# Second block's expert outputs: gated at the PSUM copy and added to the output rows by the scatter, in place of a separate combine

## What is computed

```python
h2 = rms_norm(x, norm_ffn[l])
x = x + hier_moe_2(h2, ...)

# hier_moe_2: group softmax picks 1 of 4 groups, then the best 2 of its 8 experts
weights = g_p[:, None] * e_p                      # one gate for each of a token's two experts
combine = jnp.sum(one_hot(expert_idx) * weights[..., None], axis=1)
for e in range(32):
    he = silu(hf @ w_gate[e]) * (hf @ w_up[e])    # 1024 -> 256
    y = y + combine[:, e:e+1] * (he @ w_down[e])  # 256 -> 1024
```

## Time and profile before

| | us |
|---|---|
| median of 3 runs (1504.05 to 1507.62) | 1504.61 |
| the profiled execution, its own time | 1505.68 |
| span of the profiled execution | 1503.8 |
| TensorE busy in the span | 1288.5 (86%) |
| VectorE, ScalarE, GpSimd busy | 703.1, 462.1, 421.1 |
| mean DMA rate over the span | 174 GB/s |
| mean granted TensorE clock | 0.925 of full |

### The profile page before, as it was taken

How to read it: one execution, slowest core, us unless ns; L and a number is a source line. 1 busy time by engine, 2 the same in 40 slices (tenths; PEclk the granted TensorE clock), 3 DMA queues, 4 the chain that set the end, 5 groups by cost and what they waited for, 6 DMA issues and landing times. The chain is left out here.

```text
span 1503.8 us, 20161 instructions
## 1 busy us (share of the span) xinstructions
PE 1288.5 (86%) x7568; PEld 1030.9 (69%) x7568; DVE 703.1 (47%) x1271; ACT 462.1 (31%) x1011; POOL 421.1 (28%) x358
## 2 busy tenths in 40 slices
PE   7997789949999439899999999999888948999782
PEld 6776467839999329778989978788676844554440
DVE  5797773634343474763762636673124351111112
ACT  4542343223233144443242243433222311111110
POOL 5355211211010205312423324134323302332213
PEclk9999779959999769999999999999989968999996
DMA  7300350169996422301221303322113489999995
GB/s 265 112 0 1 129 208 31 42 245 379 373 387 249 131 88 77 113 1 32 87 71 71 112 30 112 115 64 77 56 58 115 184 356 364 418 419 419 419 385 184
DMA packets 65285, 262.33 MB, mean 174 GB/s; under 512 B 8456, under 2 KB 18312, under 8 KB 52384
## 3 DMA queue, kind: packets, MB, share of 16 engines
q1 hardware_dynamic: 54176, 233.73, 40.5%
q0 software_dynamic: 9216, 21.00, 4.0%
q10 hardware_dynamic: 1792, 6.29, 1.2%
HBM read 242.04 MB, written 29.43 MB: 181 GB/s over the span
## 5 line engine op out<-in xcount | busy, mean ns | idle before, releaser
L1703 POOL TENSOR_TENSOR block_w_lo<-block_w,block_w_hi 128x512 fp32r<-128x512 f32 x96 | 130.4, 1361 | 219.8 <-ACT block_w_hi L1681 219.8
L241 PE MATMUL dil_bank<-block_w_hi,xT_hi 128*128 128x512 f32 x288 | 116.8, 406 | 4.3 <-PEq L830 4.3
L2380 PE MATMUL e_gu<-e_w,e_xT 128*64 128x256 f32 x896 | 105.8, 390 | 15.3 <-DMA e_w<-in_gu 14.6
L1681 ACT ACTIVATE block_w_hi<-block_w 128x512 fp32r<-128x512 f32 x96 | 60.4, 631 | 182.9 <-PE dil_bank L243 117.5
L242 PE MATMUL dil_bank<-block_w_lo,xT_hi 128*128 128x512 f32 x288 | 115.0, 399 | 0.0
L243 PE MATMUL dil_bank<-block_w_hi,xT_lo 128*128 128x512 f32 x288 | 114.9, 399 | 0.0
L2380 PEld LDWEIGHTS e_gu<-e_w,e_xT 128*64 128x64 f32 x896 | 63.9, 140 | 48.9 <-DMA e_w<-in_gu 16.5
L241 PEld LDWEIGHTS dil_bank<-block_w_hi,xT_hi 128*128 128x128 f32 x288 | 77.6, 269 | 8.8 <-issue 4.7
L242 PEld LDWEIGHTS dil_bank<-block_w_lo,xT_hi 128*128 128x128 f32 x288 | 77.8, 270 | 4.0
L243 PEld LDWEIGHTS dil_bank<-block_w_hi,xT_lo 128*128 128x128 f32 x288 | 77.6, 269 | 4.3
L2442 DVE TENSOR_TENSOR e_prod<-e_sg,e_gu 128x128 f32<-128x128 f32 x32 | 9.2, 287 | 140.4 <-ACT e_sg L2473 140.4
(11 more groups left out here) (506 smaller groups left out, 3116.1 us busy)
## 6 DMA issues: line engine op xcount, KB each, us to landing
e_w<-in_gu SPq DMA_DIRECT2D x44, 2048.0 KB, 18.0
e_w<-in_dn SPq DMA_DIRECT2D x48, 1024.0 KB, 19.9
block_w<-in_w_dil SPq DMA_DIRECT2D x9, 2048.0 KB, 8.1
block_w<-in_w_out SPq DMA_DIRECT2D x4, 2048.0 KB, 9.0
block_w<-in_w_gates SPq DMA_DIRECT2D x4, 2048.0 KB, 9.0
w_t<-in_w_in_t SPq DMA_DIRECT2D x12, 512.0 KB, 3.5
slot_rows<-blank SPq DMA_DIRECT2D x12, 512.0 KB, 6.3
slot_rows<-e_y ACTq DMA_DIRECT2D x16, 384.0 KB, 8.9
```

The lines of the kernel that those rows point to most:

```text
L241: pe.matmul(out, lhs[0], rhs[0], start=first, stop=False)
L1681: act.activation(wh[:, j % RING, 0:width[i]], k.w[:, slot, c, 0:width[i]], ACT.Copy).then_inc(hi_ready, 1)
L1703: pool.tensor_tensor(wl[:, j % RING, 0:width[i]], k.w[:, (q0 + i) % 2, c, 0:width[i]], wh[:, j % RING, 0:width[i]].bitcast(F32), ALU.subtr ...
L2380: ins = pe.matmul(gubank[t % 2][g * S:(g + 1) * S, 0:2 * FG], xT[t % 2][:, turned_at(c):turned_at(c) + S], w1_piece(slot.of[t], w, 2 * FG) ...
```

## The change

1. `out_rows` of the second block: GpSimd stores each finished residual tile to `out` (four DMAs of 512 KB), with a semaphore `residual_out`.
2. `route`: `y_of` with its three VectorE steps goes. The `tok_of` step is moved ahead of the six steps for `slot`, `exp_of` and `used`. New is `gate_of`, the gate of each slot: two VectorE multiplies, 32 small matmuls with the one-hot tables that `tok_of` was made from, and a copy.
3. ScalarE's copy from PSUM takes `gate_of` as its scale.
4. The scatter goes to `out` by `tok_of` and adds (`compute_op=ALU.add`). A token can stand in two tiles, so scatter t now waits until scatter t - 1 has landed, where it waited for t - 2; scatter 0 waits for the residual.
5. `Combine` is deleted: no `slot_rows` gathers, no adds, no final store by SyncE. The block ends when the last two scatters have landed.

```diff
@@ out_rows, GpSimd
+                if residual is not None:
+                    for tt in range(TT):
+                        pool.wait_ge(row_ready, tt + 1)
+                        pool.dma_start(residual[tt * P:(tt + 1) * P, :], x1[:, tt, :]).then_inc(k.residual_out, 16)
@@ route, TensorE
+                if k.gate_of is not None:
+                    pe.wait_ge(hot_ready, 2)
+                    for j in range(2 * TT):
+                        i, tt = divmod(j, TT)
+                        for g in range(GROUPS):
+                            ins = pe.matmul(gbank[g * S:(g + 1) * S, 0:NT], ohr[:, i, tt, :], hot[:, i, tt, :], start=(j == 0),
+                                            stop=(j == 2 * TT - 1))
+                    ins.then_inc(gates_done, 1)
@@ route, VectorE: tok_of is taken here, ahead of slot, exp_of and used
-                if k.y_of is not None:
-                    step(dve.tensor_scalar(empty[:], tbank[:, 0:NT], -0.5, float(NO_ROW), ALU.is_gt, ALU.mult))
-                    step(dve.scalar_tensor_tensor(empty[:], k.c("iota")[:, 0:NT], 2.0 * S, empty[:], ALU.mult, ALU.add))
-                    step(dve.tensor_scalar(k.y_of[:], empty[:], k.c("half_row"), None, ALU.add))
+                if k.gate_of is not None:
+                    for i in range(2):
+                        dve.tensor_tensor(hot[:, i], hot[:, i], bc(k.gate[:, i], 2, NT), ALU.mult).then_inc(hot_ready, 1)
+                    dve.wait_ge(gates_done, 1)
+                    step(dve.tensor_copy(k.gate_of[:], gbank[:, 0:NT]))
@@ experts_moving, GpSimd
                     pool.wait_ge(y_s, t + 1)
-                    if t >= 2:
-                        pool.wait_ge(y_out[t % 2], 16 * (t // 2))
-                    pool.indirect_dma_start(halves, bass.IndirectOffsetOnAxis(ap=k.y_of[:, t:t + 1], axis=0), y[t % 2][:],
-                                            None, bounds_check=GROUPS * SLOTS - 1, oob_is_err=False).then_inc(
-                                                y_out[t % 2], 16)
+                    if t >= 1:
+                        pool.wait_ge(y_out[(t - 1) % 2], 16 * ((t - 1) // 2 + 1))
+                    else:
+                        pool.wait_ge(k.residual_out, 16 * TT)
+                    pool.indirect_dma_start(sums, bass.IndirectOffsetOnAxis(ap=k.tok_of[:, t:t + 1], axis=0), y[t % 2][:],
+                                            None, bounds_check=GROUPS * SEQ - 1, oob_is_err=False,
+                                            compute_op=ALU.add).then_inc(y_out[t % 2], 16)
@@
-                pool.sem_inc(tail.stored, 1)
-                tail.gather(pool)
@@ experts_moving, VectorE, ScalarE, SyncE
-                tail.add(dve)
-                    act.activation(y[t % 2][:], ybank[t % 2][0:U, :], ACT.Copy).then_inc(y_s, 1)
+                    act.activation(y[t % 2][:], ybank[t % 2][0:U, :], ACT.Copy, scale=k.gate_of[:, t:t + 1]).then_inc(y_s, 1)
-                tail.store(sp)
```

More of the change, by code:

```diff
@@ L1323, in row_stats, with out_rows @@
     return dve.bn_stats(stats[:, half, :], x[:, half * 512:(half + 1) * 512])
-def out_rows(k, name, src, xT, tmp, vecs, loads, router, lg, rows, finished, scale=None, gain_cols=None, early=None, over_rows=None):
+def out_rows(k, name, src, xT, tmp, vecs, loads, router, lg, rows, finished, scale=None, gain_cols=None, early=None, over_rows=None, residual=None):
     nc, x1 = k.nc, k.x1
@@ L1818, in route @@
         ohj = k.sb(s, f"{name}_ohj", [P, 2, TT, NT])
[L1819 to L1822, removed]
+        hot = k.sb(s, f"{name}_hot", [P, 2, TT, NT])
+        rbank, totals, tbank, gbank = (k.ps(s, f"{name}_{n}") for n in ("rbank", "totals", "tbank", "gbank"))
+        (step_d, diff_ready, exp_ready, m_ready, rank_done, oh_ready, tok_done, bits_ready, xg_ready, tok_ready, hot_ready,
+         gates_done) = (
+            k.sem(f"{name}_{n}") for n in ("step", "diff", "exp", "mready", "rank", "oh", "tok", "bits", "xg", "tokready",
+                                           "hot", "gates"))
         with nc.Block() as block:
@@ L2240, in __init__, with experts_moving @@
         self.last = [max([u for u in range(t) if self.of[u] == self.of[t]], default=None) for t in range(NT)]
-def experts_moving(k, name, E, S, x_in, rows, w_gu, w_dn, out_rows, weights, late, tail):
+def experts_moving(k, name, E, S, x_in, rows, w_gu, w_dn, out, weights, late):
     nc = k.nc
@@ L2486, in _ @@
                 every_tile(act, used, tile)
[L2489 to L2497, removed]
-        for j in range(2 * TT):
-            k.gathered[4 + j] += 16
-    def gather(self, pool):
-        pool.wait_ge(self.stored, 1)
-        for j in range(2 * TT):
-            tt, i = divmod(j, 2)
-            pool.indirect_dma_start(self.rows[j], None, self.out_rows, bass.IndirectOffsetOnAxis(
-                ap=self.k.slot[:, i, tt:tt + 1], axis=0)).then_inc(self.row_in[j], 16)
-    def add(self, dve):
-        x = self.x
-        for tt in range(TT):
-            for i in range(2):
-                j = 2 * tt + i
-                dve.wait_ge(self.row_in[j], self.row_base[j] + 16)
-                dve.scalar_tensor_tensor(x[:, tt, :], self.rows[j], self.k.gate[:, i, tt:tt + 1], x[:, tt, :],
-                                         ALU.mult, ALU.add).then_inc(self.used, 1)
-                dve.wait_ge(self.used, j + 1)
-    def store(self, sp):
-        for tt in range(TT):
-            sp.wait_ge(self.used, 2 * tt + 2)
-            sp.dma_start(self.out[tt * P:(tt + 1) * P, :], self.x[:, tt, :]).then_inc(self.out_done, 16)
-        sp.wait_ge(self.out_done, 16 * TT)
 class CombineAndNorm:
@@ L3282, in second_block @@
                  early=load_early,
-                 over_rows=load_over_rows)
+                 over_rows=load_over_rows, residual=d["out"])
     stage.close()
@@ L3307, in second_block @@
         w1.append([k.w1_over_consts, k.sb(s, "e2_w1_6b", [P, 3 * 2 * FF])])
-        experts_moving(k, "e2", E2, S2, k.gather_sems[2:4], d["rows"], d["gu2"], d["dn2"], slots, weights, late,
-                       Combine(k, "c2", slots, w1[2:4], k.x1, d["out"]))
+        experts_moving(k, "e2", E2, S2, k.gather_sems[2:4], d["rows"], d["gu2"], d["dn2"], d["out"], weights, late)
 def first_block(k):
```

32 lines of the change are left out of this document (15 added, 17 removed).

## The result

| | before | after |
|---|---|---|
| median, us | 1505.91 | 1546.38 |
| lowest and highest | 1504.05 to 1507.62 | 1543.73 to 1554.63 |
| runs on the same chip | 4 | 4 |
| profiled execution, its own time | 1505.68 | 1546.12 |

The ratio is 1.027, with a 95% interval of 1.0243 to 1.0297: 40 us slower, where 6 or 7 were forecast and 1487 to 1560 was the range. The new wait does what the forecast said of it, but several of the numbers around it were too small. The time lies in the range because the range was drawn wide enough for the slow-add rival too; the forecast's own case was 1504 to 1524.

What follows compares the result with a forecast made beforehand. The prediction took the experts as bound by weight loads, then by scatters in series: 1315 + 22 P, with P = 8.85 after removing the combine, gives span 1509.8; plus 1.9 it is 1511.7, said as 1512, range 1487 to 1560.

Steps and rivals of the forecast that it cites:

- slow-add rival: Expert scatters: reading, adding and writing take 2 to 3 us more each, P about 11, time 1559; above 1524, chance 0.25.
- the forecast's own case: Scatters in series set the experts' pace: P 8.5 to 9.4, 1504 to 1524 us, residual delay included; chance 0.50.
- What bounds the kernel before: Experts' stage: it ends with the weights, the last arriving at 1466.7, with the DMA engines full from 1254 to 1460.
- What goes: End of the kernel: the combine is all on the path, 24.2 us; if nothing else moved, the span would be about 1480.
- The new wait: Expert scatters: each waits for the one before, so the period is landing plus about 0.8 us, 9.2 at full load.
- P: Period from one expert scatter to the next in series, taken as 8.85 us; each 0.1 us is 2.2 us of time.
- The discount for gaps in the load: Expert scatters: engines idle 8% of the time let waiting scatters land early, so P drops from 9.2 to 8.85 us.
- The addition in the engines: DMA engines during the experts: an add also reads its destination, 0.3 us a tile, 10 us over 32.
- third rival: DMA engines: the add's read costs twice 0.3 us a tile but no latency; P 8.8 or more, 1511 to 1518.
- The residual store: Before the experts: 2.1 MB, 5.1 us, hides in two later DMA gaps of 3.7 and 2.2 us; without them 5 us.
- Scatters do not bind: Expert scatters: landings average below 7.2 us, P below 8.0, weights set the end; 1482 to 1500 us, chance 0.25.
- The fourth: Before the experts: the residual store holds up `token_rows` by its full 5 us with no gap, shifting everything to 1517.

Runs made afterwards that it cites:

- b_add: The kernel before with the scatter adding to slot_rows instead of copying, old wait for t - 2 and combine kept: 1519.06 us, ratio 1.0074.
- a_turns: The changed kernel with experts taken in turn from the four groups, so scatter t waits for t - 2 only: 1503.14 us, ratio 0.9965.
- b_serial: The kernel before with only the wait changed: plain scatter t waits for scatter t - 1, combine kept: 1534.05 us, ratio 1.0173.
- a_plain: The changed kernel without the addition: scatters copy to the output rows, still in series: 1521.87 us, ratio 1.0087.
- b_serial_add: The kernel before with both the adding scatter and the wait for t - 1, combine kept: 1560.33 us, ratio 1.0354.
- a_turns_serial: The changed kernel with experts in turn from the four groups, but the wait for t - 1 kept: 1548.94 us, ratio 1.0257.
- a_turns_no_residual: a_turns without the four residual stores and scatter 0's wait for them, so the output lacks the residual: 1503.02 us, ratio 0.9969.
- a_late_residual: The changed kernel with the residual stores moved into the routing, behind the gathers of tiles 0 and 1: 1549.63 us, ratio 1.0281.
- a_turns_all: a_turns_nowait plus left residual halves stored early by SyncE, which also waits for the last two scatters: 1499.88 us, ratio 0.995.
- a_turns_nowait: a_turns without SyncE's wait for the first gathered rows ahead of its last three first loads: 1503.41 us, ratio 0.9971.
- a_sp_end: The changed kernel with SyncE instead of GpSimd waiting for the last two scatters: 1543.82 us, ratio 1.0229.

## Why the forecast was right in direction and short in size

**What bounds the kernel before.** Right, by the way back: with two scatters allowed in flight and the addition in, the chain ends in weights again (b_add, a_turns), and the addition's DMA price of 13 us shows up there as 11 us of time.

**What goes, 24.2 us.** Right, as far as three pairs of runs can tell: one kernel of each has the combine, the other the residual store and the gates. What was gained, plus scatter 0's later place behind the last residual add, plus the new end of about 5 us: 12 + 4 + 5 from b_serial to a_plain, 13 + 6 + 6 from b_serial_add to after, 16 + 6 + 5 from b_add to a_turns, that is 21 to 27 us.

**The new wait.** The mechanism is right and is shown: alone it costs 26 us (b_serial); with adding scatters, all else equal, 46 (a_turns_serial against a_turns). "Landing + about 0.8" is 0.88. The plain period was taken as 8.9 at full load: measured 8.79 and 8.76. What was sized wrong is the next term, an adding scatter's landing. The forecast's + 0.3 us, near the plain rows "since queueing dominates", was + 1.0 (8.76 to 9.82, 8.79 to 9.73). That is 0.7 us of P, some 15 us of time. Of it, 0.58 is GpSimd's own: 1.59 us for the instruction where the earlier trace rows have 1.01. The rest is flight. It is there with the weights in as well, where a landing is 4.0 instead of the 2.9 of the earlier trace rows, of which again 0.58 is issue; it also puts scatter 31 later, as scatter 30 took 4.5 us to land.

The Trainium skill's fit (page "DMA: Bandwidth & Descriptors", section "Anatomy of one DMA — SWDGE (gpsimd) path") of 2.0 us plus bytes / 436e3 gives 2.3 us for 0.13 MB, an estimate. The adding scatters of after do not agree with it even when almost alone: 3.7 at least.

**The discount for gaps in the load.** The second wrong term: 9.2 was lowered to 8.85, because the engines would be idle 8% of the time and a waiting scatter would land early then. That is 0.35 us of P, 8 us of time. The idle share was overrated. By the same reckoning b_serial, 8.2 us of DMA work in a period of 8.79, should have gaps of 7%, and it has none (share 1.00). It moved 411 GB/s x 8.79 us = 3.6 MB in a period, not 3.41; by these bytes the weights of about 23 tiles go out during the 22 periods. In after it is 371 GB/s x 9.82 us, 3.6 MB again, or 9.1 us of work at b_add's 401 GB/s, an estimate, where the forecast had 8.5. So b_serial says nothing on what a gap is worth.

The gaps in after are real (0.96 busy, 371 GB/s), but do not shorten the flights evenly. The 22 steps go 12.2, 12.3, 11.7, 9.8, 6.8, 10.7, 7.1, 11.4, 7.6 and so on, long and short in turn. It is the long ones, above anything in the of before, that carry the mean. b_serial_add shows the same pattern; the plain scatters of b_serial do not (10.4, 8.5, 8.2, 8.2, 8.1, 7.3, 8.7). With such steps a median says little: it is 9.5 in after and 7.0 in b_serial_add, at periods of 9.82 and 9.73; the mean landing, period less 0.88, is 8.9 in both. The landings of b_serial_add up to 1455:

```profile
DMA to landing us min/median/max: 6.0/7.0/10.7
```

One reading is that a scatter which lands early lets a gather and a tile through, whose freed buffers bring a burst of loads in front of the next scatter. That was argued from the order of events and is not shown; no run fixed the load.

**The addition in the engines.** 0.3 us a tile was 0.41, in the third rival's direction. In after, where the engines are busy 0.96, it does not set the end; it is what b_add pays.

**Behind the wait.** "Gather n + 2 is queued behind scatter n - 3", 12.4 us to the down projection, then tiles at TensorE's pace: this held, 46.75 forecast and 45.8 measured.

**The residual store.** "They hide there", and "net zero, within 1" for the routing, together a start as before: wrong, it is 6.0 us later (6.6 with the shift of the whole kernel). There were gaps of 3.7 and 2.2 us, and the store fills both. But a gap is no free place if something behind it in the same queues is late by what fills it. `token_rows` lands later, the loads behind it go out at 1229.77 instead of 1225.49, and the backlog, which held the start already, ends at about 1249 instead of 1245. The forecast had each piece ("without that cover they would be 5 us"), and put the loads' delay "inside the second gap". a_turns_no_residual shows it is the stored bytes and not the routing; a_late_residual, that moving them behind the gathers does not help (46.8 instead of 44.1 to the first turn); a_turns_all, that moving half of them ahead into an idle stretch does (39.4). What event exactly releases the engines then stays open; a_turns_nowait excludes SyncE's wait for the gather.

**The end.** Not in the sum at all: 5.6 us lie behind the last landing, where the kernel before has next to nothing. Moving the wait to SyncE leaves 4.0 of them in the profile of a_sp_end and 5.0 in a_turns_all.

**Rivals.** Scatters do not bind: falls, mean landing 8.9 where it needed less than 7.2. Slow add: the time, 1546, lies in this case's field, above 1524, which had a chance of 0.25; by mechanism it is half as much as that case had (P 9.82 instead of about 11), and the rest of the way came mostly from the start and the end. The forecast's own case, P 8.5 to 9.4 and 1504 to 1524 with a chance of 0.50, failed by its own sign. The fourth, the residual store holding up `token_rows`, happened as well, in addition to the rest and not in its place: terms of the same sign added up, where the forecast had treated them as alternatives. That the 1546 fell inside the range is owed to the width given for rivals, not to the sum: of the 34.5 us missing in the span, 21 are the period, 7 the start and 6 the end.

## What to carry to other kernels

A wait that puts small DMAs in series beside a saturating stream costs landing plus 0.9 us each, here 8.8 us plain and 9.5 to 9.8 adding, while the same DMAs with two in flight keep up with 7 us a tile at an even longer flight. So look for an order in which neighbours touch different rows before paying for the wait (46 us between a_turns_serial and a_turns).
The rule that makes the wait necessary for neighbours that do share rows is in the Trainium skill, page "DMA: Bandwidth & Descriptors", section "Rules for kernel authors": an accumulate reads its destination and writes later, and what another DMA wrote between is lost. No run here leaves that wait out where neighbours share rows.
A gap in the DMA share covers a store only if nothing queued behind it starts later; a stretch that was idle altogether, before the weights, did cover half of it (a_turns_all); and the sum has to go on to the end of the program, past the last landing.

## What the runs showed of the hardware

An adding scatter holds GpSimd for 1.59 us, a plain one for 1.01. By b_add it takes 0.41 us more of the 16 DMA engines for 0.13 MB, though its read is not in the bytes moved. With such scatters in the mix the engines, fully busy (1.02), moved 401 GB/s instead of 419 (b_add, 1270 to 1450). Adding scatters beside the weights land after a median of 11.4 us (a_turns; 11.2 in b_add) with two in flight, and after 8.9 on average one at a time; plain ones after a median of 8.1 with up to two in flight. And where an adding GpSimd scatter is the last work, the span ends 9.2 to 9.5 us behind its issue with GpSimd waiting for it (11.2 once), 7.8 and 8.8 with SyncE waiting, of which its landing explains 3.8.
